# First attention of a two-block network on one core: where its score blocks, turned blocks and the mirrored sums of the stage behind it are placed

## The reference, cut to what matters

```
s = einsum("bhmqd,bhmkd->bhmqk", q, k) * 64 ** -0.5     # two maps m per head
a = softmax(s)
w = a[:, :, 0] - lam * a[:, :, 1]
o = einsum("bhqk,bhkd->bhqd", w, v)
...
u = short_conv(hx @ w_hy, hy_conv_w, hy_conv_b)           # three taps over the rows
v, x1, x2 = split(u)
z = v
for n, gate in enumerate((x1, x2)):
    z = gate * (long_conv(z, k_f[:, n]) + hy_skip[n] * z)
```

## Time and profile before

| | |
|---|---|
| median of 3 runs | 3250.12 us (3246.41 to 3250.49) |
| the profiled execution | 3249.94 us, its span 3248.1 us |
| busy PE, DVE, ACT, POOL | 3100.0 (95%), 2312.6 (71%), 1304.0 (40%), 800.5 us (25%) |
| the first attention in the span | from 505.8 us (first score matmul) to 740.8 us (last block turned back) |
| first matmul of the Hyena stage | 751.4 us |
| mean granted TensorE clock of the run | 0.981 of full speed |

### The profile page before, as it was taken

How to read it: one execution, slowest core, us unless ns; L and a number is a source line. 1 busy time by engine, 2 the same in 40 slices (tenths; PEclk the granted TensorE clock), 3 DMA queues, 4 the chain that set the end, 5 groups by cost and what they waited for, 6 DMA issues and landing times.

```text
span 3248.1 us, 37697 instructions
## 1 busy us (share of the span) xinstructions
PE 3100.0 (95%) x14546; PEld 2423.2 (75%) x14546; DVE 2312.6 (71%) x3089; ACT 1304.0 (40%) x2124; POOL 800.5 (25%) x826
## 2 busy tenths in 40 slices
PE   7999998998999899999999999998899989999999
PEld 3577786667787788888877888855567877888787
DVE  6654455876646987778888666587644599989896
ACT  5431114662123433334454333376631344444443
POOL 1211101212111234321001344313544123433101
PEclk9999999999999999999999999999999999999999
DMA  6433352107645222227333345531123422222823
GB/s 225 154 139 119 135 204 81 46 1 259 208 155 175 91 91 78 85 87 283 107 127 118 104 130 176 173 128 39 40 70 123 156 79 90 85 78 78 295 88 110
DMA packets 118299, 406.86 MB, mean 125 GB/s; under 512 B 13704, under 2 KB 16328, under 8 KB 113642
## 3 DMA queue, kind: packets, MB, share of 16 engines
q1 hardware_dynamic: 65626, 200.42, 19.2%
q0 software_dynamic: 52496, 204.04, 17.7%
HBM read 321.50 MB, written 82.90 MB: 125 GB/s over the span
## 4 chain that ended last, share of the span: by engine, by line
PE 63%; DVE 8%; ACT 2%; issue 2%; POOL 1%; DMA 0%; POOLq 0%; ACTq 0%; DVEq 0%
PE PS L455 20%; PE PS L457 19%; PE PS L456 19%; PE PS L3351 2%; DVE HL L411 1%; POOL Sc L3606 1%; PE PS L3373 1%; PE PS L3390 1%; ACT HL L393 0%; ACT E L3435 0%; PE PS L3007 0%; DVE HT L1992 0%; DVE E L3530 0%; ACT Sc L3437 0%; DVE H L3658 0%
## 5 line engine op out<-in xcount | busy, mean ns | idle before, releaser
L455 PE MATMUL PS<-H,HL 128*128 128x512 f32 x1920 | 762.1, 397 | 15.2 <-DVE H L3658 7.2
L457 PE MATMUL PS<-H,HL 128*128 128x512 f32 x1920 | 752.8, 392 | 0.0
L456 PE MATMUL PS<-H,HL 128*128 128x512 f32 x1920 | 752.5, 392 | 0.0
L393 ACT ACTIVATE HL<-RAW 128x512 fp32r<-128x512 f32 (+1 forms) x429 | 312.0, 728 | 622.4 <-PE PS L457 561.4
L411 DVE TENSOR_TENSOR HL<-RAW,HL 128x512 fp32r<-128x512 f32 (+1 forms) x429 | 401.1, 935 | 146.9 <-ACT HL L393 137.4
L455 PEld LDWEIGHTS PS<-H,HL 128*128 128x128 f32 x1920 | 363.8, 189 | 105.0 <-issue 20.0
L456 PEld LDWEIGHTS PS<-H,HL 128*128 128x128 f32 x1920 | 363.9, 190 | 76.9 <-issue 2.6
L457 PEld LDWEIGHTS PS<-H,HL 128*128 128x128 f32 x1920 | 363.2, 189 | 76.8
L455 PE MATMUL PS<-HT,HL 128*128 128x512 f32 x720 | 282.6, 393 | 17.9 <-DVE rows L2314 15.8
L457 PE MATMUL PS<-HT,HL 128*128 128x512 f32 x720 | 281.5, 391 | 0.0
L456 PE MATMUL PS<-HT,HL 128*128 128x512 f32 x720 | 281.5, 391 | 0.0
(11 more groups left out here) (464 smaller groups left out, 5640.0 us busy)
## 6 DMA issues: line engine op xcount, KB each, us to landing
RAW<-in_w_up SPq DMA_DIRECT2D x100, 512.0 KB, 3.6
RAW<-in_w_down SPq DMA_DIRECT2D x82, 512.0 KB, 3.8
RAW<-in_w_proj SPq DMA_DIRECT2D x48, 512.0 KB, 3.6
scr_hid<-hidr POOLq DMA_DIRECT2D x36, 512.0 KB, 2.9
RAW<-in_w_wmodr SPq DMA_DIRECT2D x32, 512.0 KB, 4.4
HL<-in_w_dfwd POOLq DMA_DIRECT2D x16, 1024.0 KB, 6.8
HL<-in_w_dinv POOLq DMA_DIRECT2D x16, 1024.0 KB, 5.4
RAW<-in_w_wout SPq DMA_DIRECT2D x26, 512.0 KB, 4.4
```

Of the source, the lines that this page charges most:

```text
L393: e.activation(part_slot(k, p)[0], src, ACT.Copy).then_inc(*k.high.mark(j, x))
L455: e.matmul(out, lh, rh, start=first, stop=False, skip_group_check=goes_on)
L456: e.matmul(out, lh, rl, start=False, stop=False, skip_group_check=goes_on)
L457: return e.matmul(out, ll, rh, start=False, stop=last, skip_group_check=goes_on)
```

## The change

- In the attention's PE loop, T(it-1, 2) goes to the columns 256 to 511 of bank 2 (`turn_at`), beside the 256 columns of scores there, and stands between V's key blocks 6 and 7 instead of behind S(it+2). It waits for max(it+1, 0), and S(it+2)'s chunk in bank 2 waits for its copy. ACT copies it right after exp(it+1, 0).
- The last projection block hy 11 moves from banks 2 and 3 to banks 6 and 7, and S(0) is put between its two halves; S(1) follows it directly. `modx` is read before hy 11's second half. ACT runs exp(0, 0) and exp(0, 1) before hy 11's middle tap; DVE runs max(0, ·), factor(0), w(0), max(1, ·) before hy 11's side taps. The wait for the stores (`hyena_stored`) moves to ACT's first copy of a turned block, to DVE's max(2, 0) and to the head of POOL's loop.
- For the first convolution, the eight plus and minus halves are all formed by POOL, one in each of its loop's steps g = 1 to 8, out of a new buffer `z0` (two tiles, loaded by SP inside the attention) into a new buffer `mirror`. `z` is no longer loaded.
- Their 32 transposes go into the attention's last four iterations, bank by bank (`MIRROR_AT`, `MIRROR_BANK`: two banks in iteration 30, two in 31, one in 32, three in 33), with ACT's high parts in the same iterations and DVE's low parts one iteration later. R(15) comes behind the first step of the forward transform, and POOL's loads of the first two kt tiles go before its last low part.
- The second convolution keeps its order.

```diff
@@ pairs_qkv
-    order += [("hy", n) for n in range(12)]
+    order += [("hy", n) for n in range(11)]
...
+    return {**{key: 2 * ((first + n) % 3) for n, key in enumerate(order)}, ("hy", 11): 6}
@@ pe_qkv, in the loop over n and its halves h
             if n == 0:
                 rope(7, h)
+            elif n == 11 and h == 0:
+                scores1(k, e, free, 0)
...
+        if n == 10:
+            free[7] = [s.dve.at("modx")]
@@ pe_att1
+def scores1(k, e, free, j):
+    s, h, t = k.att1, j // 8, j % 8
+    e.wait_ge(*k.in_head[h % 2].at(h, 2))
+    for c, (a, b) in enumerate(CHUNKS):
+        for m in range(2):
+            for x in free[3 * m + c]:
+                e.wait_ge(*x)
+            r = slice(64 * m, 64 * m + 64)
+            x = e.matmul(k.PS[:, 3 * m + c, 0:b - a], k.q1[r, h % 2, blk(t)], k.k1[r, h % 2, a:b], start=True, stop=True)
+            free[3 * m + c] = [s.dve.at("max", j, m)]
...
     def turn(j, c):
-        claim(6)
+        b, at, n = turn_at(c)
+        claim(b)
         e.wait_ge(*s.dve.at("w", j))
...
-    scores(0)
-    scores(1)
-    for it in range(36):
+    scores1(k, e, free, 1)
+    for it in range(34):
...
         if 2 <= it < 34:
-            values(it - 2, [4, 5, 6, 7, 8, 9])
+            values(it - 2, [4, 5, 6])
+        if 1 <= it < 33:
+            turn(it - 1, 2)
+        if 2 <= it < 34:
+            values(it - 2, [7, 8, 9])
...
         if it + 2 < 32:
-            scores(it + 2)
-        if 1 <= it < 33:
-            turn(it - 1, 2)
+            scores1(k, e, free, it + 2)
+        for b in MIRROR_AT.get(it, []):
+            mirror_turns(k, e, free, b)
+MIRROR_BANK = [0, 1, 3, 4, 5, 2, 3, 4]
+MIRROR_AT = {30: [0, 1], 31: [2, 3], 32: [4], 33: [5, 6, 7]}
+def mirror_turns(k, e, free, b):
+    s, bank = k.hyena, MIRROR_BANK[b]
+    for c in range(4):
+        e.wait_ge(*s.pool.at("plus" if b < 4 else "minus", 0, c))
+    for x in free[bank]:
+        e.wait_ge(*x)
+    for c in range(4):
+        x = e.transpose(k.PS[:, bank, blk(c)], k.mirror[:, c, blk(b)], k.ident[:, :])
+    x.then_inc(*s.pe.mark("turn", 0, 3, b))
+    free[bank] = [s.dve.at("p_lo", 0, b)]
+def turn_at(c):
+    return (6, 0, 4) if c < 2 else (2, 256, 2)
@@ act_att1
     for m in range(2):
         exponents(0, m)
-    for it in range(36):
+    hyena_middle(k, e, 11)
+    for it in range(34):
         if 1 <= it < 33:
             turn(it - 1, 0)
         if it + 1 < 32:
             exponents(it + 1, 0)
+        if 1 <= it < 33:
+            turn(it - 1, 2)
...
+        for b in MIRROR_AT.get(it, []):
+            mirror_high(k, e, 0, b)
@@ dve_att1
-    after(e, *k.qkv.every())
-    for n in range(6, 12):
-        e.wait_ge(*k.st_ev[k.slots_qkv["hy", n][0]].at("hy", n))
+    e.wait_ge(*k.qkv.pool.at("rcos", 7))
+    e.wait_ge(*k.qkv.pe.at("hy", 9))
...
     for it in range(34):
+        if it == 0:
+            factor(0)
+            combine(0)
         if it + 1 < 32:
             most(it + 1, 0)
             most(it + 1, 1)
-        if it < 32:
+        if it == 0:
+            hyena_sides(k, e, 11)
+        elif it < 32:
             factor(it)
...
+        for b in MIRROR_AT.get(it - 1, []):
+            mirror_low(k, e, 0, b)
@@ pool_att1
+    hyena_stored(k, e)
+    for g in range(16):
         if g in (4, 8):
             load_head(k, e, g // 4 + 1)
+        if 1 <= g < 9:
+            mirrored((g - 1) // 2, "minus" if (g - 1) % 2 else "plus")
+        scaled(g)
         if g:
             low(g - 1)
+    load_k(k, e, 0, 0)
+    load_k(k, e, 0, 1)
+    low(15)
@@ pe_hyena, after the matmuls of a forward step
+            if o == ft == 0:
+                rows_out1(k, e, free, 15)
@@ sp_hyena
-    e.wait_ge(*k.att1.pe.at("turn", 31, 2))
     for c in range(4):
-        e.dma_start(k.z[:, c, :], k.d_hy[c]).then_inc(*k.in_z[c].mark(0))
+        if c >= 2:
+            e.wait_ge(*k.hyena.pool.at("minus", 0, c - 2))
+        e.dma_start(k.z0[:, c % 2, :], k.d_hy[c]).then_inc(*k.in_z[c].mark(0))
```

More of the change, by code:

```diff
@@ L1238, in claim @@
             e.wait_ge(*x)
[L1240 to L1250, removed]
     def turn(j, c):
-        claim(6)
+        b, at, n = turn_at(c)
+        claim(b)
         e.wait_ge(*s.dve.at("w", j))
-        n = 4 if c < 2 else 2
         for q in range(n):
-            x = e.transpose(PS[:, 6, blk(q)], weights_of(k, j, 0)[:, blk(4 * c + q)], k.ident[:, :])
+            x = e.transpose(PS[:, b, at + 128 * q:at + 128 * q + 128], weights_of(k, j, 0)[:, blk(4 * c + q)], k.ident[:, :])
         x.then_inc(*s.pe.mark("turn", j, c))
-        free[6] = [turned1(k, j, c)]
+        free[b] = [turned1(k, j, c)]
     def values(j, kbs):
@@ L1307, in turn_out1, with act_rows_out1, act_high1, hyena_stored @@
 def turn_out1(k, j, c):
-    n = 4 if c < 2 else 2
-    return k.WT1[:, j % 2, 4 * c:4 * c + n, :], k.PS[:, 6, 0:128 * n].rearrange("p (k n) -> p k n", k=n)
+    b, at, n = turn_at(c)
+    return k.WT1[:, j % 2, 4 * c:4 * c + n, :], k.PS[:, b, at:at + 128 * n].rearrange("p (k n) -> p k n", k=n)
+def act_rows_out1(k, e, g):
+    s = k.att1
+    e.wait_ge(*s.pe.at("out", g))
+    if g >= 2:
+        e.wait_ge(*s.pool.at("o_lo", g - 2))
+    e.activation(k.OT1[:, g % 2, :], k.PS[:, 7, 256:512], ACT.Copy, scale=k.lamb[:, 4:5]).then_inc(*s.act.mark("out", g))
+def act_high1(k, e, g):
+    s = k.att1
+    e.wait_ge(*s.act.at("out", g))
+    e.activation(k.H[:, 0, g // 4, blk(g % 4, 256)], k.OT1[:, g % 2, :], ACT.Copy).then_inc(*s.act.mark("o_hi", g))
+def hyena_stored(k, e):
+    after(e, *k.qkv.every())
+    for n in range(6, 12):
+        e.wait_ge(*k.st_ev[k.slots_qkv["hy", n][0]].at("hy", n))
 def act_att1(k, e):
@@ L1456, in low, with mirrored, load_k @@
                         ALU.subtract).then_inc(*s.pool.mark("o_lo", g))
-    for g in range(17):
+    def mirrored(c, name):
+        if name == "plus":
+            e.wait_ge(*k.in_z[c].at(0))
+        z = k.z0[:, c % 2, :]
+        to = k.mirror[:, c, blk(int(name == "minus"), 512)]
+        e.tensor_tensor(to, z[:, 0:512], z[:, 1023:511:-1], ALU.add if name == "plus" else ALU.subtract).then_inc(*k.hyena.pool.mark(name, 0, c))
+    hyena_stored(k, e)
+    for g in range(16):
         if g in (4, 8):
             load_head(k, e, g // 4 + 1)
-        if g < 16:
-            scaled(g)
+        if 1 <= g < 9:
+            mirrored((g - 1) // 2, "minus" if (g - 1) % 2 else "plus")
+        scaled(g)
         if g:
             low(g - 1)
+    load_k(k, e, 0, 0)
+    load_k(k, e, 0, 1)
+    low(15)
+def load_k(k, e, o, ft):
+    s, q = k.hyena, ft % 2
+    if ft >= 2:
+        e.wait_ge(*s.dve.at("q", o, ft - 2))
+    elif o:
+        e.wait_ge(*(s.pe.at("turn", o, 2) if ft == 0 else s.pe.at("turn", o, 3, 7)))
+    else:
+        e.wait_ge(*k.att1.pool.at("o", 15))
+        e.wait_ge(*k.att1.dve.at("w", 31))
+        e.wait_ge(*k.att1.act.at("o", 31))
+    e.dma_start(k.kt[:, q, :], k.d_K[8 * o + ft]).then_inc(*k.in_kt[q].mark("k", o, ft))
 def mirror_slot(k, c):
@@ L1482, in pe_hyena @@
     for o in range(2):
-        for c, banks in [(0, range(6)), (1, range(6)), (2, range(6)), (0, (6, 7)), (1, (6, 7)), (2, (6, 7)), (3, range(8))]:
+        for c, banks in [(0, range(6)), (1, range(6)), (2, range(6)), (0, (6, 7)), (1, (6, 7)), (2, (6, 7)), (3, range(8))] if o else []:
             e.wait_ge(*s.dve.at("plus", o, c))
-            e.wait_ge(*(s.pool.at("minus", 0, c) if o == 0 and c < 3 else s.dve.at("minus", o, c)))
+            e.wait_ge(*s.dve.at("minus", o, c))
             for b in banks:
@@ L1492, in pe_hyena @@
                 x.then_inc(*s.pe.mark("turn", o, c))
-        for b in range(8):
+        for b in range(8) if o else []:
             free[b] = [s.dve.at("p_lo", o, b)]
@@ L1541, in act_hyena @@
     s, PS, H, QR = k.hyena, k.PS, k.H, k.QR
+    unit = k.unit_hyena
+    act_rows_out1(k, e, 15)
+    act_high1(k, e, 15)
     after(e, *k.att1.every())
[L1543 removed]
     for o in range(2):
[L1545 to L1550 removed]
+        for b in range(8) if o else []:
+            e.wait_ge(*s.pe.at("inv", 0, 3))
+            mirror_high(k, e, o, b)
         for ft in range(8):
@@ L1589, in dve_hyena @@
     z, tp, kt = k.z, k.tp, k.kt
-    after(e, *k.att1.every())
     unit = k.unit_hyena
@@ L1679, in pool_hyena @@
     z, tp, kt, H = k.z, k.tp, k.kt, k.H
-    after(e, *k.att1.every())
-    def load_k(o, ft):
-        q = ft % 2
-        e.wait_ge(*(s.dve.at("q", o, ft - 2) if ft >= 2 else s.pe.at("turn", o, 2) if ft == 0 else s.pe.at("turn", o, 3, 7)))
-        e.dma_start(kt[:, q, :], k.d_K[8 * o + ft]).then_inc(*k.in_kt[q].mark("k", o, ft))
-    for c in range(3):
-        e.wait_ge(*k.in_z[c].at(0))
-        e.tensor_tensor(mirror_slot(k, c)[:, 512:1024], z[:, c, 0:512], z[:, c, 1023:511:-1], ALU.subtract).then_inc(*s.pool.mark("minus", 0, c))
     for o in range(2):
-        load_k(o, 0)
-        load_k(o, 1)
+        if o:
+            load_k(k, e, o, 0)
+            load_k(k, e, o, 1)
         for ft in range(8):
```

111 lines of the change are left out of this document (53 added, 58 removed).

## The result

The changed kernel takes 3210.22 us (median of 4 runs, 3207.54 to 3212.68), the kernel before 3248.26 us (4 runs beside it, 3241.34 to 3250.49). The ratio is 0.9886, with an interval of 0.9868 to 0.9905, or about 37 us less. The forecast was 3211 (3202 to 3224).

What follows compares the result with a forecast made beforehand. PE, busy 95% of the first attention's span, was taken as the bound. Regular part 19, head 7 and tail 13 sum to 39 us off 3249.9, giving 3211 us, range 3202 to 3224.

Steps and rivals of the forecast that it cites:

- Regular part: Attention loop: T(·, 2) leaves bank 6, period 6.63 becomes 5.94, 0.69 saved in each of 28 iterations, 19 us taken.
- third rival: Attention loop: T(·, 2) or the scores wait as long as T(·, 0) did; only head and tail gain, 3230; chance 0.06.
- second rival: Attention loop: DVE becomes the bound by later starts or POOL's sums meeting w; time about 3220; chance 0.13.
- The fourth: Attention loop: new waits let PE's clock fall to 1.2 GHz; slower, 3266 with ten such iterations; chance 0.03.
- POOL's sums: Attention loop: POOL's eight sums run beside DVE's maxima, which read PSUM, and cost others 0 us.
- the other end: POOL's sums in the loop: eight collisions with w at 1.0 us each, less the margin of about 0.3, cost 6 us.
- Head: Start of the attention: T(1, 0) comes at 525.2 instead of 533.17; 7 us taken, ends 3 and 9.
- the store was seen 3.4 us behind the last tap: Head: hy 11's last side tap ends at 516.2, so its store is seen at 519.6.
- first rival: Half clock in the head and ACT's queue in the tail: both at low ends, 30 us saved, 3220; chance 0.14.
- ACT's table: Head: ACT's middle tap behind Exp needs no table reload, 0; at most 2 x 1.28 us if it does.
- Tail: T(29, 0) to the first forward matmul: 19.2 instead of 32.6 us; 13 taken, ends 8 and 15.
- Sum: Whole kernel: 19 + 7 + 13 = 39 us off the profiled 3249.9, giving 3211; chance 0.62.

Runs made afterwards that it cites:

- Experiment 1: Kernel before with only T(·, 2) in bank 2 and between the values, head and tail as before; 3221.54 us, ratio 0.9935.
- experiment 5: Changed kernel with T(·, 2) in its new place between the values but in bank 6 as before; 3256.48 us, ratio 1.0018.
- experiment 4: Changed kernel with POOL's eight sums pushed by a wait to meet DVE's w; 3209.87 us, ratio 0.9899.
- experiment 3: Changed kernel with SP's z0 loads waiting for the stores of the last projection; 3207.33 us, ratio 0.9883.
- experiment 2: Kernel before with hy 11 in banks 6 and 7, S(0) between its halves, moved waits, z loaded behind the attention; 3237.81 us, ratio 0.9977.
- experiment 9: Experiment 3 run again, the changed kernel with z0 reads behind the stores, beside the changed kernel; 3209.11 us, ratio 0.989.
- experiment 6: Changed kernel with all eight banks of mirrored turns in iteration 33, none in 30 to 32; 3215.40 us, ratio 0.9896.
- experiment 8: Changed kernel again, nothing edited; 3210.67 us, ratio 0.9881.
- experiment 10: Changed kernel once more, nothing edited, side by side with experiment 9; 3207.52 us, ratio 0.9884.

## Why the prediction was right, step by step

**Regular part: right, in size and mechanism.** 5.94 was forecast and 5.939 measured, (697.05 - 530.76) / 28. Every check of the forecast can be read in the trace: max(·, 0) is released by the scores and starts 0.1 behind T(·, 0) (602.00 against 601.91), where I had 0.3; ACT's copy of T(·, 2) ends at 605.26, long before S asks for it. w started at 605.76 and ended at 607.30 for a T(·, 0) at 607.75, a margin of 0.45 where I had 0.34. Experiment 1 shows that the move alone gives it, experiment 5 that it fails without the bank. The third rival, one ring of waits for another, is what experiment 5 shows, and there it costs 1.5 per iteration (7.5 less 5.94); the change escapes it since T(·, 2) has a place of its own. The second rival did not occur in the loop: w was never over 1.55, and PE has no wait. The fourth, a clock that falls, did not either: it is 1.00 throughout the loop.

**POOL's sums: 0 was right, the other end was too large.** I took 6 us (the stretch of 1.0 in the earlier trace rows, eight times, less the margin). With all eight sums made to meet w, experiment 4 shows 1.3. The error was to read the DVE rows of 1.7 as a symmetric stretch of two operations: it is the second one that waits, and what it waits is at most what is left of the first. The Trainium skill (SBUF — State Buffer, Who interferes with whom) says just this, that the two kinds of instruction exclude each other, and the rows of experiment 4 agree: a sum of 1.28 took 1.23 more behind w's rest of 1.38, and w took 0.70 more behind a sum's rest of 0.90. They do not agree with the 10 us that I worked out by that page, which took the whole POOL operation for each of the eight. In the change as it is, sums beside a maximum, which reads PSUM, took 1.28, as the page's rule has it. Two of the eight, behind the loads of the next head on POOL, began inside w and took 2.58 and 2.59; w kept its 1.54.

**Head: the mechanism was right, the size was off; the term that failed is "the store was seen 3.4 us behind the last tap".** I took that duration from the earlier trace rows, where the store had the queues nearly to itself. The change moves SP's reads of z in front of the attention, and they wait for the same last side tap: two reads of 512 KB at 516.92, the store at 517.06. The store then lands in 6.3 us. Transfers of the head in the changed kernel, 505 to 530 us: queue, count, KB each, median us from issue to landing.

```profile
z<-scr_hy SPq DMA_DIRECT2D x2, 512.0 KB, 5.6
scr_hy<-Xp POOLq DMA_DIRECT2D x1, 512.0 KB, 6.3
```

I counted these reads only for the weights queued behind them on SP and not for what they take from the store. It cost 3.3 us directly, and PE's rest grew from the 4 that I foresaw to 6.7. Behind it the clock was 0.50 and S(3) took 5.15 where it takes 2.42 at full clock: 2.7 more, and I had allowed 1.5. The wait is undone by experiment 3, and by experiment 2 from the other side, so it is shown that the reads cause it. The table reads stand behind the store in all these runs, and whether the transfers meet in the DMA engines (share 1.04 from 520 to 523) or in the DRAM no run separates. The forecast of T(1, 0) at 525.2, taken from an S(0) at 500.3, is close to the 525.34 of experiment 3, but partly by luck: the forecast had full clock there, the run had 1.4 of half clock in S(3), and experiment 9 takes 26.8 where 24.9 was forecast. The first rival named half clock behind the store's wait, and that part of it occurred; the queue on ACT in the tail that it also wanted did not.

The 3.0 itself is loose. The head before, 32.9, ran the last ten matmuls of each of its first three groups of scores at half clock (4.02 in the earlier trace rows, then 4.07 and 4.11), and experiment 1 took 2.0 less for the same head by its clock. The changed kernel's head took 28.6 to 30.1 in five traces with the reads beside the store (the change, experiments 4, 6, 8 and 10). Against a head before at that better clock the saving would be an estimated 1 (30.9 less 29.9), and without the reads beside the store 4 to 6 (30.9 less 26.8 or 25.1).

**ACT's table: 0 extra loads, as taken.** The one load (1.28, at 494.97) is before S(0), and the middle tap at 509.06 runs between the exponentials of block 0 and block 1 with none beside it. The Trainium skill (ScalarE: Activation LUTs, Table sets) says that identity is in every set; this trace agrees.

**Tail: right in the length after, and the saving partly luck.** 19.2 was forecast, 18.9 measured. The saving, 13 forecast and 13.6 read, is counted from the 32.6 of a trace with 1.6 of half clock in one iteration (experiment 2); against a tail before at full clock there it is 12.0. The waits are the ones named, at other sizes: 1.11 for w(30) where I had 1.4, 0.69 for ACT's copy where I had 0.7. The clock is 1.00 from 697 to 716. The next table of the forward transform is issued at 723.65 behind R(15)'s low part, and no forward step waits for it.

**Sum.** The three parts, 19.4, 3.0 and 13.6, are 36.1 in the traces before rounding, against 39. The other 1.2 us of the 37.3 between the two profiled executions lie outside the stretch, within what that part scatters by itself. So the sum was 3 too large, by the head. That the time fits to 1 us is partly luck: the kernel before measured 3248.26 beside the change, 1.7 less than the 3249.94 that the forecast started from, and the half clock in the tail of the trace before gave another 1.6 that the forecast had not counted on.

## What to carry to other kernels

A group that closes a ring of waits in each iteration is worth a look at the spare columns of banks that other groups use only in part; it is the bank that frees the ring, and the same move without one costs more than it brings. When a wait for a transfer stays in the plan, write down every DMA that any queue issues at the same moment, those of the moved steps above all; its duration from before holds only with the company that it had before. Of two operations that exclude each other, price only what is left of the first when the second starts, less the margin. Before a saving of 1 to 3 us is read from a pair of traces, look at the granted clock of the same stretch in both.

## What was not expected of the hardware

- A store of 512 KB from POOL's queue took 2.9 us without reads beside it and 6.1 to 6.4 when two reads of 512 KB from SP's queue were issued in the same moment (six traces); with the reads behind it, it took 2.9 again. Three table reads of 1 MB issued behind it on its own queue made no difference: the store of hy 10, with none behind it, took 2.9 too.
- With the reads behind the store they meet the table reads instead: they take 10.3 to 10.6 us where they took 5.1 to 5.6. Nobody waits for them there.
- After the same rest of 2.0 us on PE, one execution of the same program ran S(3) in 3.77 us and another in 5.42: how long the half clock (0.50, 1.2 GHz) lasts behind a rest is not the same from run to run. Whether it comes is not the same either. Behind the same rests of 1.6 and 0.3, S(2)'s last ten matmuls took 2.41 in four traces (experiments 2, 8, 10 and the change) and 3.93 to 4.11 in four others (experiments 3, 4, 5 and 9), with the same instructions on PE up to there.
